# Experts' rows by indexed DMA through a table in memory, in place of gather and scatter matmuls

## The chip, the cores and the metric

One core of a Trainium2 chip runs the whole program. The metric is the device time of one execution, in microseconds. PE is the matrix engine, DVE the vector engine, ACT the scalar engine, POOL the general engine that here clears buffers and issues small loads, SP the engine that issues the weight loads. Each engine runs its own list of instructions in order and waits for the others through semaphores.

## The reference

Two layers over 256 frames of width 1024. Each has a token mixer and a channel mixer; the channel mixer of the second layer is a top-2-of-8 expert SwiGLU, and that is where the change lies:

```python
logits = (xf @ w_router) + b_router
top_logit, top_idx = lax.top_k(logits, 2)
top_w = softmax(top_logit)
# for every expert e, over the rows routed to it:
out = (silu(xb @ w1[e]) * (xb @ w3[e])) @ w2[e]      # 1024 -> 3584 -> 1024
y[token] += out * weight_of_that_row                  # each token is in two experts
x = layer_norm(alpha * x + (1 + gate) * y)
```

There are 512 routed rows in all; how many an expert gets is known only on the chip.

## The kernel before, in words

**Weights.** All weights stream from memory in pieces of 1 MB (w_raw, a ring of 6) on SP's queue. For each piece ACT rounds a high part (w_hi, L755 in the expert stage, L498 before) and DVE subtracts to get the low part (w_lo, L1300, or L878); both have 3 slots, freed when PE has used the piece (split_used). A product is three matmuls, high by high, low by high, high by low (L1426 to L1428). A ring slot is free again once DVE has made the low part (piece_used).

**Experts.** The stream of one expert is 42 pieces: 7 panels of A (w1), B (w3) and C (w2), two pieces each. The three engines run a loop over 8 experts and branch on the expert's row count: over 192 rows, 129 to 192 ("packed"), 65 to 128, and up to 64 ("few"). Up to 128 rows are one block, more are two. In the packed and few forms the low part of a 64-row half sits in the partitions 64 to 127 beside the high part, so that one matmul serves both, and the sums of both halves are added later. For C this is the product of L1432 and L1433; an expert of 65 to 128 rows has the extra matmuls of L1953.

**Rows in and out.** The normalised rows are kept as h_hi and h_lo. DVE builds 0/1 matrices (pick, L1268, and pick_w with the routing weight, L1269). PE gathers the rows of a block with 16 products from h_hi and 16 from h_lo (L1871), which come out turned as the next operand; ACT and DVE copy them to actT_hi (L741) and actT_lo (L1276). After an expert ACT and DVE copy its sums to hbuf (L845, L1385); early in the next expert, between its second and third piece, PE scatters them with 8 matmul instructions per block (L1880), and DVE adds the result to yacc (L1284). pick_w is turned on PE (L1914) to place. An expert opens its 2 or 4 sum banks with products of zeros (L1944), after its fourth piece.

**Order around the change.** At an expert's end PE runs: turn of the last panel (L1925), gather for the next expert (L1871), wait for gT (ACT L779, then DVE L1323 or L1327), the last two C pieces, and, next expert, A, A, scatter, B, turn of pick_w, B, zeros. The order is written out by hand in each engine's program; nothing is planned at run time but the branches on the count.

**The start of the program.** In the first token mixer every second piece is a modulation piece, which DVE multiplies into mod_acc (L905). mod_acc is first cleared by POOL (L441 to L443) and gets its bias by a small load on POOL's queue (L449); the first modulation piece waits for that load (semaphore acc_ready). DVE takes pieces in the order of the stream.

Of the kernel before, what the change touches and what calls it, by code (L numbers as in the profile page):

```python
# [23 lines left out]
F32 = mybir.dt.float32  # L24
# [38 lines left out]
CONSTS = C_IOTA + SEQ  # L63


def constants():

    c = np.zeros((P, CONSTS), np.float32)
# [118 lines left out]
DVE_MIX_STEPS, DVE_DENSE_STEPS, DVE_ROUTE_STEPS = 39, 22, 32  # L187
# [16 lines left out]
def trunk(nc, I, consts, out):  # L204
    with ExitStack() as ctx:
# [52 lines left out]
        h_lo = sb("h_lo", [P, TT, D], F32R, scope=ffn)  # L258
        h_hi = sb("h_hi", [P, TT, D], F32R, scope=ffn)
# [6 lines left out]
        pick = sb("pick", [P, TT, SEQ], F32R, scope=ffn)  # L266
# [6 lines left out]
        wsel = sb("wsel", [P, TT, EXPERTS + 1], scope=ffn)  # L273
        ffn.close()

        ps = ctx.enter_context(nc.psum_tensor("ps", [P, 8, BANK], F32))

        gT_end_hi, gT_end_lo = (h_hi[:, part, 0:BANK].rearrange("p (b c q) -> p b c q", b=2, q=P) for part in range(2))
# [23 lines left out]
        acc_free, acc_zero, yacc_zero = sem("acc_free"), sem("acc_zero"), sem("yacc_zero")  # L302
# [30 lines left out]
        hh_ready, hl_ready = sem("hh_ready"), sem("hl_ready")  # L333
# [4 lines left out]
        gathered_hi = [sem(f"gathered_hi{b}") for b in range(2)]  # L338
        gathered_lo = [sem(f"gathered_lo{b}") for b in range(2)]
# [98 lines left out]
        def _(gp):  # L438
# [20 lines left out]
            gp.dma_start(cst[:, C_PAST:], consts[:, C_PAST:]).then_inc(tables_loaded, 16)  # L459
            for layer in range(DEPTH):  # L460
# [29 lines left out]
        def _(act):  # L490
# [58 lines left out]
            def route_norms(sub, n, held, ahead):  # L549

                def high_h(t):
                    A(h_hi[:, t, :], hbuf[:, t, :], ACT.Copy).then_inc(hh_ready, 1)

# [7 lines left out]
                high_h(0)  # L561
                root(n + 4, 1)
                ahead(2)
                keep_turned(sub, 1, held)
                high_h(1)
# [14 lines left out]
            for layer in range(DEPTH):  # L580
# [149 lines left out]
                else:  # L730
# [8 lines left out]
                    def gathered_rows(b, n, first_bank=4):  # L739
                        act.wait_ge(gathered_hi[b], n)  # L740
                        A(actT_hi[:, :, b * P:(b + 1) * P],  # L741
                          ps[:, first_bank:first_bank + 2, :].rearrange("p c (k q) -> p (c k) q", q=P), ACT.Copy).then_inc(xg_hi_ready[b], 1)

                    gathered_rows(0, 1)
                    with nc.Fori(0, EXPERTS, engines=[act.engine], hint_back_edge=True, head_slot={act.engine: 0}) as e:
                        count = act.value_load(counts_i[0:1, bass.ds(e, 1)], min_val=0, max_val=SEQ)

                        def expert(blocks, packed=False, few=False):
# [33 lines left out]
                            def places():  # L782
                                act.wait_ge(place_sent, e + 1)
                                ins = A(place[:, 0:blocks, :], ps[:, 0, 0:blocks * SEQ].rearrange("p (b q) -> p b q", q=SEQ), ACT.Copy)
                                if packed or few:
                                    half = blocks - 1
                                    ins.then_inc(place_copied, 1)
                                    act.wait_ge(place_copied, e + 1)
                                    ins = A(place[HALF_P:P, half, :], ps[0:HALF_P, 0, half * SEQ:(half + 1) * SEQ], ACT.Copy)
                                else:  # L790
                                    act.sem_inc(place_copied, 1)
# [4 lines left out]
                            if blocks == 2:  # L796
                                gathered_rows(1, e + 1)
                            else:
                                act.sem_inc(xg_hi_ready[1], 1)
# [5 lines left out]
                            places()  # L805
# [27 lines left out]

                            def tail(last):
                                gT_part(panel_0 + NP)
                                if not last:
                                    round_at(12, loads6, done6)
                                    if blocks == 1:
                                        gathered_rows(0, e + 2, 6)
                                    round_at(13, loads6, done6)  # L840
                                    if blocks == 1:
                                        round_at(14, loads6, done6)
                                act.wait_ge(split_used, done0 + (EXPERT.n_split + SPLIT))
                                for b in range(blocks):
                                    ins = A(hbuf[:, b, 0:BANK], bank(2 * b), ACT.Copy)  # L845
                                ins.then_inc(y_act, 1)
                                if not last and blocks == 2:
                                    round_at(14, loads6, done6)
                                    gathered_rows(0, e + 2)
# [21 lines left out]
        def _(dve):  # L871
# [157 lines left out]
            dve.sem_inc(added, 4)  # L1029
# [12 lines left out]
            for layer in range(DEPTH):  # L1042
# [173 lines left out]
                else:  # L1216
# [3 lines left out]
                    def low_h(t):  # L1220
                        dve.wait_ge(hh_ready, t + 1)
                        TTn(h_lo[:, t, :], hbuf[:, t, :], h_hi[:, t, :].bitcast(F32), ALU.subtract).then_inc(hl_ready, 1)

                    low_h(0)
                    rest_of_piece(EXPERT, 0, sbase + MIX.n_split)
                    wide = [P, TT, EXPERTS]
# [18 lines left out]
                    TTn(gap, m2, m1, ALU.subtract).then_inc(gap_ready, 1)  # L1245
                    dve.wait_ge(e2_ready, 1)
# [3 lines left out]
                    step(TTn(tmp, is1, w1.broadcast_to(wide), ALU.mult))  # L1250
                    step(TTn(is2, is2, w2.broadcast_to(wide), ALU.mult))

                    nc.vector.memset(wsel[:, :, EXPERTS:], 0.0)
                    nc.vector.memset(posm[:, :, EXPERTS:], -1.0)
                    step(TTn(wsel[:, :, 0:EXPERTS], tmp, is2, ALU.add))
                    low_h(1)
                    dve.wait_ge(pos_sent, 1)

                    step(STT(pos, ps[:, ROUTE + 1, 0:16].rearrange("p (t e) -> p t e", t=TT), 1.0, sel, ALU.add, ALU.mult))
                    step(TS(posm[:, :, 0:EXPERTS], pos, -1.0, None, ALU.add))  # L1260
                    nc.vector.tensor_copy(counts_i[:, 0:EXPERTS], ps[:, ROUTE + 1, 16:24]).then_inc(counts_ready, 1)
# [3 lines left out]
                    def pick_tokens(e):  # L1265
                        for t in range(TT):
                            at = posm[:, t, bass.ds(e, 1)]
                            TS(pick[:, t, :], iota, at, None, ALU.is_equal)  # L1268
                            ins = TS(pick_w[:, t, :], iota, at, wsel[:, t, bass.ds(e, 1)], ALU.is_equal, ALU.mult)  # L1269
                        ins.then_inc(pick_ready, 1)  # L1270
# [3 lines left out]
                    def gathered_rows(b, n, first_bank=6):  # L1274
# [775 lines left out]
```

## Time and profile before

| | us |
|---|---|
| three runs | 1778.58, 1779.21, 1779.35 |
| median | 1779.21 |
| span of the profiled execution | 1779.2 |

| engine | busy us | share of the span |
|---|---|---|
| PE | 1695.2 | 95% |
| DVE | 1375.4 | 77% |
| ACT | 1026.8 | 58% |
| POOL | 36.7 | 2% |

The page gives no other time for the profiled execution than its span, which is that of the median run. In this view a matmul's busy time overlaps the next one's, so a run of n matmuls is read from the start of the first to the start of what follows. Waits are put down to the semaphore that came last. The DMA share is the busy share of the core's 16 DMA engines.

### The profile page before, as it was taken

The numbers are of one execution on the slowest core, as the hardware profiler recorded it, in microseconds if no ns is written. First come the engines' busy times: TensorE is split into PE (matmuls) and PEld (weight loads), VectorE is DVE, ScalarE is ACT, GpSimd is POOL, SyncE is SP. The second block draws the span as 40 slices with busy tenths as digits, with TensorE's granted clock in tenths as the row PEclk, the third lists the DMA queues.
The fourth block names the chain that finished last, engine by engine and source line by source line (L and its number), as shares of the span: only waits on it lengthen the run. The fifth ranks groups of instructions, "written<-read, shape, count | busy, mean of one in ns | idle before, by whom it ended". The sixth has DMA issues, their size and how long they took to land.

```text
span 1779.2 us, 21351 instructions
## 1 busy us (share of the span) xinstructions
PE 1695.2 (95%) x7542; PEld 1306.9 (73%) x7543; DVE 1375.4 (77%) x1171; ACT 1026.8 (58%) x823; POOL 36.7 (2%) x40
## 2 busy tenths in 40 slices
PE   5999899999999898999999999999899999999995
PEld 2587758887677766777877778887677777787773
DVE  5686868676786886888888966656488889888887
ACT  1375433433465335777767765454477777777772
POOL 1100010000100000000000000000000000000000
PEclk9999999999999998999999999999999999999998
DMA  9885459774685246999999976666499999999992
GB/s 358 306 319 180 154 180 333 279 260 142 245 295 172 97 175 243 384 377 339 369 329 342 386 285 214 212 213 234 138 371 394 335 378 385 336 370 359 341 379 84
DMA packets 210530, 502.24 MB, mean 282 GB/s; under 512 B 9137, under 2 KB 13409, under 8 KB 210481
## 3 DMA queue, kind: packets, MB, share of 16 engines
q1 hardware_dynamic: 208770, 496.15, 77.5%
q0 software_dynamic: 1712, 5.43, 1.0%
q8 instruction: 32, 0.52, 0.1%
q14 instruction: 16, 0.13, 0.0%
HBM read 500.50 MB, written 1.05 MB: 282 GB/s over the span
## 4 chain that ended last, share of the span: by engine, by line
PE 84%; DVE 9%; issue 4%; DMA 2%; ACT 1%; DVEq 0%; SPq 0%; ACTq 0%
PE ps L1426 20%; PE ps L1428 19%; PE ps L1427 19%; PE ps L1432 5%; PE ps L1433 5%; PE ps L1437 4%; DVE w_lo L1300 3%; PE ps L1880 2%; PE ps L1953 2%; PE ps L1871 2%; PE ps L1925 2%; DMA w_raw<-in_w_mod_mix_dram 1%; DVE gates L1095 1%; DMA w_raw<-in_w_in_dram 1%; PE ps L1488 1%
## 5 line engine op out<-in xcount | busy, mean ns | idle before, releaser
L1300 DVE TENSOR_TENSOR w_lo<-w_raw,w_hi 128x2048 fp32r<-128x2048 f32 x333 | 757.9, 2290 | 197.3 <-ACT w_hi L755 195.4
L755 ACT CAST w_hi<-w_raw 128x2048 fp32r<-128x2048 f32 x333 | 635.9, 1910 | 199.7 <-PE ps L1433 107.3
L1426 PE MATMUL ps<-w_hi,actT_hi 128*128 128x512 f32 (+1 forms) x1464 | 584.2, 399 | 31.7 <-issue 11.2
L1428 PE MATMUL ps<-w_hi,actT_lo 128*128 128x512 f32 (+1 forms) x1464 | 567.3, 387 | 0.0
L1427 PE MATMUL ps<-w_lo,actT_hi 128*128 128x512 f32 (+1 forms) x1464 | 566.8, 387 | 0.0
L1426 PEld LDWEIGHTS ps<-w_hi,actT_hi 128*128 128x128 f32 x1464 | 277.0, 189 | 103.4 <-issue 26.6
L1428 PEld LDWEIGHTS ps<-w_hi,actT_lo 128*128 128x128 f32 x1464 | 276.9, 189 | 57.6
L1427 PEld LDWEIGHTS ps<-w_lo,actT_hi 128*128 128x128 f32 x1464 | 277.5, 190 | 55.2 <-issue 3.3
L878 DVE TENSOR_TENSOR w_lo<-w_raw,w_hi 128x2048 fp32r<-128x2048 f32 x81 | 185.4, 2290 | 91.3 <-ACT w_hi L498 91.0
L498 ACT CAST w_hi<-w_raw 128x2048 fp32r<-128x2048 f32 x81 | 154.5, 1909 | 112.0 <-PE ps L1428 98.8
L1432 PE MATMUL ps<-w_hi,gT_hi 128*128 128x512 f32 x448 | 183.3, 409 | 4.7 <-issue 1.9
L1433 PE MATMUL ps<-w_lo,gT_hi 128*128 128x512 f32 x448 | 177.1, 395 | 0.0
L905 DVE SCALAR_TENSOR_TENSOR mod_acc<-w_raw,c_act,mod_acc 128x512 f32<-128x512 f32 x176 | 120.1, 747 | 10.5 <-DMA w_raw<-in_w_mod_mix_dram 10.5
L1432 PEld LDWEIGHTS ps<-w_hi,gT_hi 128*128 128x128 f32 x448 | 84.1, 188 | 43.7 <-issue 26.3
L1433 PEld LDWEIGHTS ps<-w_lo,gT_hi 128*128 128x128 f32 x448 | 84.2, 188 | 17.6
L1437 PE MATMUL ps<-w_raw,actT_raw 128*128 128x512 f32 x144 | 66.4, 617 | 4.8 <-DMA w_raw<-in_w_in_dram 4.0
L1437 PEld LDWEIGHTS ps<-w_raw,actT_raw 128*128 128x128 f32 x144 | 27.9, 197 | 39.5 <-issue 37.4
L1426 PE MATMUL ps<-w_hi,gT_hi 128*128 128x512 f32 x136 | 54.1, 398 | 2.2 <-DVE gT_hi L1327 2.2
L765 ACT ACTIVATE silu<-ps 128x512 f32<-128x512 f32 x56 | 33.5, 599 | 39.2 <-PE ps L1428 38.9
L1427 PE MATMUL ps<-w_lo,gT_hi 128*128 128x512 f32 x136 | 54.1, 398 | 0.0
L1428 PE MATMUL ps<-w_hi,gT_lo 128*128 128x512 f32 x136 | 53.5, 393 | 0.0
L779 ACT ACTIVATE gT_hi<-ps 128x256 fp32r<-128x256 f32 (+1 forms) x63 | 27.9, 453 | 37.0 <-PE ps L1925 37.0
(249 smaller groups left out, 1283.9 us busy)
## 6 DMA issues: line engine op xcount, KB each, us to landing
w_raw<-in_exp_w_dram SPq DMA_DIRECT2D x336, 1024.0 KB, 5.9
w_raw<-in_ffn_w_dram SPq DMA_DIRECT2D x33, 1024.0 KB, 5.3
w_raw<-in_w_mod_mix_dram SPq DMA_DIRECT2D x24, 1024.0 KB, 9.2
w_raw<-in_w_mod_ffn_dram SPq DMA_DIRECT2D x24, 1024.0 KB, 5.7
w_raw<-in_w_gate_dram SPq DMA_DIRECT2D x24, 1024.0 KB, 6.8
w_raw<-in_w_in_dram SPq DMA_DIRECT2D x14, 1024.0 KB, 6.4
w_raw<-in_w_out_dram SPq DMA_DIRECT2D x8, 1024.0 KB, 5.1
w_raw<-in_w_branch_c_dram SPq DMA_DIRECT2D x4, 1024.0 KB, 5.0
```

What stands on the lines that cost most here:

```text
L498: nc.scalar.copy(w_hi[:, j % SPLIT, :], w_raw[:, i % RING, :]).then_inc(split_hi, 1)
L755: nc.scalar.copy(w_hi[:, i % SPLIT, :], w_raw[:, i % RING, :]).then_inc(split_hi, 1)
L878: TTn(w_lo[:, j % SPLIT, :], w_raw[:, i % RING, :], w_hi[:, j % SPLIT, :].bitcast(F32), ALU.subtract).then_inc(piece_used, 1)
L905: ins = STT(acc, w[:, k, n * BANK:(n + 1) * BANK], c_act[:, 2 * (q % 4) + k:2 * (q % 4) + k + 1], acc, ALU.mult, ALU.add)
L1300: TTn(w_lo[:, i % SPLIT, :], w_raw[:, i % RING, :], w_hi[:, i % SPLIT, :].bitcast(F32), ALU.subtract).then_inc(piece_used, 1)
L1426: MM(to, hi, w_h, start=first, stop=False)
L1427: MM(to, hi, w_l, start=False, stop=False)
L1428: return MM(to, lo, w_h, start=False, stop=last)
L1432: MM(to, packed, w_h, start=first, stop=False)
L1433: return MM(to, packed, w_l, start=False, stop=last)
L1437: return MM(to, actT_raw[:, k, t * P:(t + 1) * P], w_raw[:, slot, at * width:(at + 1) * width], start=first, stop=last)
L1871: ins = MM(to, part[:, t, k * P:(k + 1) * P], pick[:, t, b * P:(b + 1) * P], start=t == 0, stop=t == 1)
```

## The change

- The rows no longer go through pick, h_hi and h_lo. A table by_row in memory (8 experts by 256 rows of 4 KB) takes each token's row once per chosen expert by 4 indexed DMAs from POOL; the row numbers are computed on DVE (row_no, row_at). An expert's rows are then loaded to xrows by two plain DMAs, and PE turns them with 8 transposes per block (turn_rows); ACT makes the high part and DVE the low part by subtraction.
- At the end of each expert but the last, the sums go to hbuf (for few and packed experts both halves are added there, through fold), and ACT issues the DMA that writes them into the same places of by_row (send_rows). After the last expert has begun, POOL fetches them with 4 indexed DMAs to yacc and xrows; DVE multiplies them by the routing weights w1 and w2. Only the last expert's rows go through place and the scatter matmuls.
- The whole table is first cleared: 16 DMAs of 512 KB each, from a block of zeros in the constants, issued by POOL before the first mixer's small loads.
- The first routing steps on DVE are reordered, PE's filler products after the count are 10 and not 2, the filler after the last expert's turn is gone, and PE waits for the rows inside the branch on the count.

On POOL, at the start of the program; cst and by_row are loaded from the constants, mod_acc's is the bias load. Before:

```order
L459 DMA cst<-constants_dram 128x1984
L462 DMA sinks_sb<-in_sinks_dram 128x8
L463 DMA pool_scale_sb<-in_pool_scale_dram 128x2x1
L466 DMA w_pool_sb<-in_w_pool_dram 64x2x64 x2
L449 DMA mod_acc<-in_b_mod_ffn_dram 1x16x192
```

And now, with the 16 clearing DMAs:

```order
L468 DMA cst<-constants_dram 128x1984 [waits piece_used]
L470 DMA by_row<-constants_dram 128x1024 x16
L473 DMA sinks_sb<-in_sinks_dram 128x8 [waits gate1_ready]
L474 DMA pool_scale_sb<-in_pool_scale_dram 128x2x1
L477 DMA w_pool_sb<-in_w_pool_dram 64x2x64 x2
L458 DMA mod_acc<-in_b_mod_ffn_dram 1x16x192 [waits acc_zero]
```

The clears stand ahead of every small load of the first mixer in the same queue (the three memsets between the last two rows are left out in both lists).

On PE, at the end of an expert of one block, from the turn of the last panel (gated) to the first matmuls of the tenth piece. Before:

```order
L1925 MATMUL ps<-cst,gated 128x128 x4
L1871 MATMUL ps<-pick,h_hi 128x128 x16
L1871 MATMUL ps<-pick,h_lo 128x128 x16
L1467 MATMUL ps<-cst 128x512 x3
L1953 MATMUL ps<-w_hi,gT_lo 128x512 x4
L1432 MATMUL ps<-w_hi,gT_hi 128x512
```

And now:

```order
L1984 MATMUL ps<-cst,gated 128x128 x4
L1938 MATMUL ps<-cst,xrows 128x128 x8
L1973 MATMUL ps<-cst,pick_w 128x128 x2
L2013 MATMUL ps<-w_hi,gT_lo 128x512 x4
L1502 MATMUL ps<-w_hi,gT_hi 128x512
```

32 gather matmuls give way to 8 transposes; the third row is the branch of the last expert in both, filler before, the turn of pick_w now.

On ACT, at the end of a few expert; raw_loaded2 stands at the rounding of the next expert's third piece. Before:

```order
L754 REGISTER_ALU [waits raw_loaded2]
L755 CAST w_hi<-w_raw 128x2048 [waits split_used]
L845 ACTIVATE hbuf<-ps 128x512 [waits split_used]
L851 UNCONDITIONAL_BRANCH
```

And now:

```order
L786 REGISTER_ALU [waits raw_loaded2]
L787 CAST w_hi<-w_raw 128x2048 [waits split_used]
L866 ISA [waits rows_sent]
L873 ACTIVATE fold<-ps 64x512 [waits split_used,y_sent_rows]
L873 ACTIVATE fold<-ps 64x512
L882 ISA [waits y_act,y_dve]
L882 DMA by_row<-hbuf 64x1024
L899 UNCONDITIONAL_BRANCH
```

One copy becomes two, and ACT now stands still for DVE (y_dve) and issues a DMA before it goes on to the next expert's pieces.

The diff, cut to its core:

```diff
@@
-DVE_MIX_STEPS, DVE_DENSE_STEPS, DVE_ROUTE_STEPS = 39, 22, 32
+DVE_MIX_STEPS, DVE_DENSE_STEPS, DVE_ROUTE_STEPS = 39, 22, 40
...
+        by_row = nc.dram_tensor("by_row", (EXPERTS * SEQ, D), F32).ap()
@@ block.gpsimd
-            gp.dma_start(cst[:, C_PAST:], consts[:, C_PAST:]).then_inc(tables_loaded, 16)
+            gp.dma_start(cst[:, C_PAST:], consts[:, C_PAST:CONSTS]).then_inc(tables_loaded, 16)
+            for n in range(EXPERTS * TT):
+                gp.dma_start(by_row[n * P:(n + 1) * P, :], consts[:, C_ZERO:C_ZERO + D]).then_inc(rows_cleared, 16)
             for layer in range(DEPTH):
...
-                    nc.gpsimd.memset(yacc[:, :, :], 0.0).then_inc(yacc_zero, 1)
                     nc.gpsimd.memset(zeros[:, :].bitcast(F32), 0.0).then_inc(zeros_set, 1)
-                    for b in range(2):
-                        gp.wait_ge(gathered_lo[b], EXPERTS)
-                    ln_rows(I["ln_ffn_g"][1], I["ln_ffn_b"][1])
+                    gp.wait_ge(rows_cleared, EXPERTS * TT * 16)
+                    gp.wait_ge(h_ready, 16)
+                    gp.wait_ge(row_at_ready, 1)
+                    for c in range(2):
+                        for t in range(TT):
+                            gp.indirect_dma_start(out=by_row[:, :], out_offset=bass.IndirectOffsetOnAxis(ap=row_at[:, c, t, :], axis=0),
+                                                  in_=hbuf[:, t, :], in_offset=None).then_inc(rows_sent, 16)
+                    gp.wait_ge(rows_sent, 4 * 16)
+                    for e in range(EXPERTS):
+                        if e:
+                            gp.wait_ge(turned[1], e)
+                            gp.wait_ge(rows_loaded[1], e * 16)
+                        for b in range(2):
+                            gp.dma_start(xrows[:, b, :], by_row[e * SEQ + b * P:e * SEQ + (b + 1) * P, :]).then_inc(rows_loaded[b], 16)
+                        if e == 0:
+                            ln_rows(I["ln_ffn_g"][1], I["ln_ffn_b"][1])
...
+                    for c, to in enumerate((yacc, xrows)):
+                        for t in range(TT):
+                            gp.indirect_dma_start(out=to[:, t, :], out_offset=None, in_=by_row[:, :], ...).then_inc(y_gathered, 16)
@@ block.scalar
+                    def turned_rows(b, n):
+                        act.wait_ge(turned[b], n)
+                        for c in range(2):
+                            ins = A(actT_hi[:, 4 * c:4 * c + 4, b * P:(b + 1) * P], bank(HW3 + 2 * c)..., ACT.Copy)
+                        ins.then_inc(xg_hi_ready[b], 1)
...
+                            def copy_sums(folds):
+                                act.wait_ge(rows_sent, 4 * 16)
+                                act.wait_ge(y_sent_rows, e * 32 + 32)
+                                act.wait_ge(split_used, done0 + (EXPERT.n_split + SPLIT))
+                                half = blocks - 1
+                                for b in range(half if folds else blocks):
+                                    ins = A(hbuf[:, b, 0:BANK], bank(2 * b), ACT.Copy)
+                                if folds:
+                                    for c in range(2):
+                                        ins = A(fold[:, c, :], ps[HALF_P:P, 2 * half + c, :], ACT.Copy)
+                                ins.then_inc(y_act, 1)
+                            def send_rows():
+                                act.wait_ge(y_dve, e + 2)
+                                act.wait_ge(y_act, e + 2)
+                                for b in range(blocks):
+                                    n = HALF_P if few or b and packed else P
+                                    act.dma_start(by_row[bass.ds(act.snap(e * SEQ + b * P), n), :], hbuf[0:n, b, :]).then_inc(y_sent_rows, 16)
@@ block.vector
+                            def copy_sums(folds):
...
+                                if folds:
+                                    dve.wait_ge(y_act, e + 2)
+                                    for c in range(2):
+                                        ins = TTn(hbuf[0:HALF_P, half, c * BANK:(c + 1) * BANK], fold[:, c, :], ps[0:HALF_P, 2 * half + c, :], ALU.add)
+                                ins.then_inc(y_dve, 1)
...
+                                rest_at(12, done6)
+                                turned_rows(0, e + 2)
+                                rest_at(13, done6)
+                                copy_sums(packed or few)
+                                rest_at(14, done6)
...
-                    add_rows(EXPERTS)
+                    dve.wait_ge(y_gathered, 4 * 16)
+                    for t in range(TT):
+                        ins = TS(yacc[:, t, :], yacc[:, t, :], w1[:, t, :], None, ALU.mult)
+                    step(ins)
+                    for t in range(TT):
+                        ins = STT(yacc[:, t, :], xrows[:, t, :], w2[:, t, :], yacc[:, t, :], ALU.mult, ALU.add)
+                    step(ins)
...
@@ block.tensor
-                    stay_busy(2, 3)
-                    pe.wait_ge(hh_ready, TT)
-                    pe.wait_ge(hl_ready, TT)
+                    stay_busy(10, 3)
                     pe.wait_ge(counts_ready, 1)
+                    def turn_rows(b, n):
+                        pe.wait_ge(rows_loaded[b], n * 16)
+                        for k in range(KD):
+                            ins = TR(ps[:, HW3 + 2 * (k // 4), ...], xrows[:, b, k * P:(k + 1) * P], ident)
+                        ins.then_inc(turned[b], 1)
...
                             turn(panel_0 + NP)
-                            if blocks == 1:
-                                with pe.If(e < EXPERTS - 1):
-                                    pe.wait_ge(pick_ready, e + 2)
-                                    gather(0, e + 2, 6, 2)
-                                with pe.Else():
-                                    stay_busy(3, 6)
+                            with pe.If(e < EXPERTS - 1):
+                                turn_rows(0, e + 2)
+                            with pe.Else():
+                                turn_places()
```

## Rows read from the trace of the kernel before

**Rows 1.** The page, the chain that ended last, its shares by engine.

```profile
PE 84%; DVE 9%; issue 4%; DMA 2%; ACT 1%; DVEq 0%; SPq 0%; ACTq 0%
```

**Rows 2.** Stretch of one few expert: us, busy per engine, clock, DMA share, GB/s.

```profile
924.00:1045.00 121.00, 118.06 (x542) 92.64 (x540) 106.19 (x67) 91.36 (x64) 0.00 (x0) 1.00 0.99 362
```

**Rows 3.** Groups by line, the packed low part of gT on DVE.

```profile
L1327 DVE TENSOR_TENSOR gT_hi<-ps,gT_hi 128x256 fp32r<-128x256 f32 x42 | 17.6, 418 | 0.0
```

**Rows 4.** Timeline of POOL, 50 to 70 us: start, duration, operation, wait before.

```profile
51.34 0.53 POOL L459 DMA_DIRECT2D cst<-constants_dram  x1 [43.65 <-DVE mod_acc L905]
...
67.62 0.52 POOL L449 DMA_DIRECT2D mod_acc<-in_b_mod_ffn_dram  x1 [0.29 <-POOL mod_acc L443]
```

**Rows 5.** DMA queues between 52 and 64 us: packets, MB, share of 16 engines.

```profile
q1 hardware_dynamic: 634, 1.42, 31.3%
q0 software_dynamic: 272, 1.09, 25.2%
```

**Rows 6.** PE and DMA in the first mixer, 80 to 90 us, as in Rows 2.

```profile
80.00:90.00 10.00, 10.00 (x54) 1.00 1.04 399
```

**Rows 7.** Timeline of SP, first and last load issued before 72.4 us.

```profile
64.29 0.37 SPq L390 DMA_DIRECT2D w_raw<-in_w_mod_ffn_dram  x1
...
71.57 0.47 SPq L390 DMA_DIRECT2D w_raw<-in_w_in_dram  x1
```

**Rows 8.** Timeline of DVE and PE at the first modulation piece of the mixer.

```profile
72.44 2.73 DVE L905 SCALAR_TENSOR_TENSOR mod_acc<-w_raw,c_act,mod_acc 128x512 f32<-128x512 f32 x4
75.09 2.28 DVE L878 TENSOR_TENSOR w_lo<-w_raw,w_hi 128x2048 fp32r<-128x2048 f32 x1
...
76.45 1.03 PE L1616 MATMUL ps<-cst,proj 128*128 128x128 f32 x8
77.43 0.50 PE L1426 MATMUL ps<-w_hi,actT_hi 128*128 128x512 f32 x1
```

**Rows 9.** PE at the start of the experts: a timeline row, then the stretch after.

```profile
673.99 0.79 PE L1426 MATMUL ps<-w_hi,actT_hi 128*128 128x512 f32 x1 [5.71 <-issue]
...
674.00:679.70 5.70, 5.70 (x13) 0.50 0.01 3
```

**Rows 10.** Timeline at the end of a few expert and the start of the next.

```profile
1381.63 1.98 PE L1871 MATMUL ps<-pick,h_hi 128*128 128x128 f32 x16
...
1385.23 0.45 PE L1432 MATMUL ps<-w_hi,gT_hi 128*128 128x512 f32 x1
...
1383.90 0.42 DVE L1327 TENSOR_TENSOR gT_hi<-ps,gT_hi 128x256 fp32r<-128x256 f32 x1
...
1391.03 0.60 ACT L845 ACTIVATE hbuf<-ps 128x512 f32<-128x512 f32 x1
1391.65 1.28 ACT L755 ACT_TABLE_LOAD   x1
1392.94 1.92 ACT L755 CAST w_hi<-w_raw 128x2048 fp32r<-128x2048 f32 x1
...
1394.51 3.60 PE L1880 MATMUL ps<-hbuf,place 128*128 128x512 f32 x8
...
1404.14 0.39 PE L1426 MATMUL ps<-w_hi,actT_hi 128*128 128x512 f32 x1
```

**Rows 11.** Timeline after the packed expert: PE begins the next one, then scatters.

```profile
1264.04 0.79 PE L1426 MATMUL ps<-w_hi,actT_hi 128*128 128x512 f32 x1 [5.51 <-issue]
...
1271.06 7.03 PE L1880 MATMUL ps<-hbuf,place 128*128 128x512 f32 x16
```

**Rows 12.** Timeline of PE after a 65 to 128 row expert: the next one begins its fifth piece.

```profile
936.59 0.39 PE L1426 MATMUL ps<-w_hi,actT_hi 128*128 128x512 f32 x1
```

**Rows 13.** Timeline of DVE at the end, and groups of like operations by line.

```profile
1761.36 0.69 DVE L1284 TENSOR_TENSOR yacc<-yacc,ps 128x512 f32<-128x512 f32 x1 [0.17 <-PE ps L1880]
...
L953 DVE SCALAR_TENSOR_TENSOR x_sb<-hbuf,rstd,lnrow 128x1024 f32<-128x1024 f32 x8 | 10.3, 1285 | 0.3
...
L1117 DVE TENSOR_SCALAR z_sb<-z_sb 128x1536 f32<-128x1536 f32 x2 | 1.9, 960 | 0.1
```

More of the change, by code:

```diff
@@ L273, in trunk @@
         wsel = sb("wsel", [P, TT, EXPERTS + 1], scope=ffn)
+        row_no = sb("row_no", [P, 8, TT, 1], scope=ffn)
+        row_at = sb("row_at", [P, 4, TT, 1], I32, scope=ffn)
         ffn.close()
+        by_row = nc.dram_tensor("by_row", (EXPERTS * SEQ, D), F32).ap()
         ps = ctx.enter_context(nc.psum_tensor("ps", [P, 8, BANK], F32))
-        gT_end_hi, gT_end_lo = (h_hi[:, part, 0:BANK].rearrange("p (b c q) -> p b c q", b=2, q=P) for part in range(2))
+        gT_end_hi, gT_end_lo = (gT_end[:, part, :].rearrange("p (b c q) -> p b c q", b=2, q=P) for part in range(2))
         assert 2 * DENSE_PANELS[-1] == BANK
@@ L337, in trunk @@
         pick_ready, place_sent, place_ready = sem("pick_ready"), sem("place_sent"), sem("place_ready")
-        gathered_hi = [sem(f"gathered_hi{b}") for b in range(2)]
-        gathered_lo = [sem(f"gathered_lo{b}") for b in range(2)]
+        turned = [sem(f"turned{b}") for b in range(2)]
         xg_hi_ready = [sem(f"xg_hi_ready{b}") for b in range(2)]
@@ L787, in places @@
                                     ins.then_inc(place_copied, 1)
[L788 to L791, printed above, removed]
+                                    act.wait_ge(place_copied, 1)
+                                    ins = A(place[HALF_P:P, half, :], ps[0:HALF_P, HW3, half * SEQ:(half + 1) * SEQ], ACT.Copy)
                                 ins.then_inc(place_ready, 1)
@@ L843, in tail @@
[L843 to L849, printed above, removed]
+                                if last:
+                                    places()
+                                    copy_sums(False)
+                                    return
@@ L1027, in _ @@
                 statistics(chain, x, t)
-            dve.sem_inc(added, 4)
             for t in range(TT):
@@ L1245, in _ @@
                     TTn(gap, m2, m1, ALU.subtract).then_inc(gap_ready, 1)
+                    dve.wait_ge(pos_sent, 1)
+                    row1, row2, off1, off2, to1, to2, was1, was2 = (row_no[:, n] for n in range(8))
+                    step(STT(pos, ps[:, ROUTE + 1, 0:16].rearrange("p (t e) -> p t e", t=TT), 1.0, sel, ALU.add, ALU.mult))
+                    step(STT(rest, number, float(SEQ), pos, ALU.mult, ALU.add))
+                    TTn(logit, is1, rest, ALU.mult)
+                    step(TTn(tmp, is2, rest, ALU.mult))
+                    RED(row1, logit, AX_X, ALU.add)
+                    step(RED(row2, tmp, AX_X, ALU.add))
+                    TS(row_at[:, 0], row1, -1.0, None, ALU.add)
+                    TS(row_at[:, 1], row2, -1.0, None, ALU.add).then_inc(row_at_ready, 1)
+                    nc.vector.tensor_copy(counts_i[:, 0:EXPERTS], ps[:, ROUTE + 1, 16:24]).then_inc(counts_ready, 1)
+                    rest_of_piece(EXPERT, 2, sbase + MIX.n_split)
                     dve.wait_ge(e2_ready, 1)
@@ L1262, in _ @@
+                    TS(row_at[:, 2], to1, -1.0, None, ALU.add)
+                    TS(row_at[:, 3], to2, -1.0, None, ALU.add).then_inc(y_at_ready, 1)
+                    TS(off1, was1, -1.0, 1.0, ALU.mult, ALU.add)
+                    step(TS(off2, was2, -1.0, 1.0, ALU.mult, ALU.add))
+                    TTn(w1, w1, off1, ALU.mult)
+                    step(TTn(w2, w2, off2, ALU.mult))
                     dve.wait_ge(counts_ready, 1)
                     moe_splits = LAYER_SPLITS + MIX.n_split
[L1265 to L1270, printed above, removed]
```

204 lines of the change are left out of this document (95 added, 109 removed).

## The prediction

> **What bounds the kernel now.** I read the chain of waits first. It runs through PE for 84% of the span [rows 1]: what comes off PE, and is not taken over by another wait, comes off the time. The granted clock and DMA share of an expert come next. In a few expert PE is busy throughout at full clock, yet the 16 DMA engines are 99% busy at 362 GB/s [rows 2]: matrix engine and weight stream end almost together. Six of the eight experts make the packed low part (42 groups over 7 panels [rows 3]); one of them is the packed one, the fourth in the timeline, so five are few and two have 65 to 128 rows. Last come the timelines of the places that the change touches: the experts' ends, where gather and scatter stand; the start of the experts; the end; and, far from the experts, the first mixer, where the 16 clearing DMAs now stand in POOL's queue.
>
> **1. The clears (the largest loss).** POOL issues its table load at 51.34 us in 0.53 us [rows 4]. Sixteen clears at about that price keep it until 60.4, so the bias load leaves near 68.9 and not at 67.6. POOL's own time is small. But the bias load stands behind 8.39 MB in one queue, and DVE's first modulation piece, at 72.44 [rows 8], waits for it. What the DMA engines must move from 52 us until then: 1.42 MB on SP's queue and 1.09 on POOL's that were moved anyway by 64 us [rows 5], the 8.39 of the clears, and the four weight pieces that SP issues between 64.29 and 71.57 [rows 7], 4.19. More weights cannot be asked for, since their slots come free behind the stalled DVE. That is 15.1 MB. At the 399 GB/s of a saturated stretch of this mixer [rows 6] it takes 37.8 us, until 90. I take 90 for the bias to land; 90 − 72.4 is 17.5 us.
> Nothing covers it. The low part that follows the modulation piece on DVE ends at 75.09 + 2.28 = 77.4, and PE's next piece begins at 77.43 [rows 8], with no slack, while PE is 10.0 of 10 us busy afterwards [rows 6], so it has nowhere to make it up. After such a pause PE comes back slow: in the experts' first stretch it had stood 5.7 us and was granted 0.50, the 1.2 GHz level, for 5.7 us [rows 9], which is 2.7 us of work lost. Sum of this step: +20. Bounds: 0, if the bias need not wait for the clears; 30, if memory-to-memory copies run at 300 GB/s instead of 399 (no row shows such a copy).
> No row tells in which order one queue is served. The Trainium skill (DMA: Bandwidth & Descriptors, section Queues, rings and completion order) says that each DMA engine takes the descriptors of a queue in ring order and alternates between queues by packets. By it the bias stays behind all clears and the step costs what stands above; were it not so, the step would be 0, which is the first rival.
>
> **2. The start of the experts.** Before, the gathers ended at 668.3, and PE then stood 5.71 us on "issue" until 673.99 [rows 9], with the new code of the loop. Now row_at is ready at about 660.5. Four indexed DMAs follow; the trace has none. Lower bound for each is the direct 0.53 us [rows 4]; I take twice that, 4.2 us for four, and for writing the last 0.52 MB 1.3 us at 399 GB/s plus an estimated 2.4 for the way: 668.5. Loading the first block back is 0.5 + 1.3 + 2.4: 672.7. Eight transposes take 1.03 us warm [rows 8], 2 cold; then the loop's code, 5.7 us again: 680.4, against 674.0. Less DVE's and ACT's parts, which fit under the code: +6. Bounds: 0 (the code comes early) and +15 (each indexed DMA takes 3 us).
>
> **3. The experts' ends, where the gain is.** Per boundary PE loses a gather, from 1381.63 until the C pieces begin at 1385.23, 3.6 us, for 1.0 us of transposes; a scatter, 3.60 less its overlapped tail of 0.6; and the turn of places, 0.3 [rows 10]. Before, these covered ACT and DVE. Between two few experts, where I follow it piece by piece:
> - gT's low part ends at 1383.90 + 0.42 = 1384.3 [rows 10]; PE, done with its transposes at 1382.9, waits. C begins at 1384.4: 0.8 of 2.6 gained.
> - C ends at 1388.05. ACT rounds the third piece (1.9) until 1390.3, copies two halves (0.6 each [rows 10]) until 1391.5, and waits for DVE's two adds, 0.69 each [rows 13], until 1392.9. Behind that wait stand its DMA issue (0.4), the table load (1.28) and the fourth piece (1.92) [rows 10]: 1396.5. Silu with its table load gives 1398.4, the fifth piece 1400.3, its low part on DVE (2.28 [rows 8]) 1402.6.
> - PE begins its fifth piece there; before it was 1404.14 [rows 10]. Gain 1.5 us of 5.8 taken off PE.
> After an expert of 65 to 128 rows ACT's copy is one, and DVE copies beside it without waiting. The same steps put the fifth piece at 932.3 and not 936.59 [rows 12]: 4.3. After the packed expert the gather stood between the sums and the 5.51 us "issue" [rows 11]; gather 4.3, scatter of two blocks 7.03 less 0.6, and places go in full: 11. Before the packed expert ACT's blocked copies come ahead of the second block's turned rows, and PE waits 6.8 us for them: gather and scatter gone, gain 1.
> Sum: 3 × 1.5 + 2 × 4.3 + 11 + 1 = 25. Bounds: all that PE is spared, 17.5 for seven gathers, 2.5 for the second block's, 24 for eight blocks' scatters, 2 for places, is 46, if ACT and DVE follow at once; 13 if every boundary but the packed one's gives only its 0.3. I take 25, near the middle, as the chains above are the rows' own.
>
> **4. Traffic.** Each expert adds 1.05 MB of rows in (both blocks always) and 0.26 to 0.8 out; at a DMA share of 0.99 [rows 2]. At an expert's head there is room while PE waits, so I take 2 us over five few experts; bounds 0 and 8 (1.3 MB by 5 at 399 GB/s is 16 us, of which the heads hide half).
>
> **5. The end.** DVE's adds ended at 1761.36 + 0.69 [rows 13], right behind PE's scatter. Now they come after two scalings (1024 columns by the 960 ns of 1536 [rows 13], 0.64 each) and two multiply-adds (1.285 each), 3.9 us, which begin with the copies done at 1757.1: 1761.1, and four adds of 0.69 end at 1763.9. Cost +2. The fetch of the rows itself starts when the last expert does, seven panels ahead.
>
> **Sum.** +20 + 6 − 25 + 2 + 2 = +5. The profiled span is 1779.2, the same as the median of the runs: 1784 us.
>
> **The rivals.**
> - *The clears hide.* The bias lands among them, or copies leave the weight queue its share, and step 1 is 0 to 4. For it: the weight queue is not busy around 60 us (1.42 MB in 12 us is 118 GB/s [rows 5]), which leaves room for some 3 MB. Against: 8.39 MB do not fit in it. Then −25 + 10 + 2 is −13: 1766, faster.
> - *ACT and DVE follow at once.* The boundaries give 40 and not 25, the clears as forecast: 1769. Against it, the chain of rows 10 has ACT's wait for DVE ahead of the fourth piece.
> - *Memory writes are slow.* The clears run at 300 GB/s or less (+30), and each indexed DMA takes 3 us (+15), the boundaries as forecast: 1779 + 30 + 15 − 25 + 4 = 1803. It decides from a clear of 1.7 us per 512 KB on.
> - *The stream of weights becomes the bound in few experts.* 45.4 MB at 399 GB/s is 114 us; they last 121 − 1.5. It would need under 380 GB/s, where 362 was moved at a 0.99 share [rows 2]: then nothing is gained there, 4.5 us less: 1789.
>
> **Chances.** Forecast 0.48 (own range 1776 to 1792), clears hidden 0.19, boundaries in full 0.10, slow writes 0.13, stream bound 0.10. Within 0.2%, 3.6 us, a measurement of this kernel can tell no change. Faster takes the first and second rival and 0.05 of the forecast's, 0.34; the same 0.11, from the forecast's lower edge; slower the rest, 0.55. Range 1764 to 1801.
>
> **What would show it.** A wait of DVE's first modulation piece on the small load near 72 us until 90, POOL's queue full of copies meanwhile, and PE at the 1.2 GHz level after it, show step 1; no such wait makes the prediction wrong and the time near 1766. PE's first expert matmul near 700 (674 + 20 + 6) shows steps 1 and 2 together. In a few expert's head, "w_hi waits for DVE" with PE waiting for w_lo at its third to fifth piece shows step 3; boundaries that shrink by 5 us make it wrong. Waits for w_raw in the expert stage would be step 4. After the last scatter DVE must be found in adds that begin 2 us later.

## The result: 45 us slower, where 5 were predicted

| | before | changed |
|---|---|---|
| median us | 1779.28 | 1824.80 |
| lowest and highest of 4 runs | 1778.58, 1781.82 | 1821.98, 1825.76 |
| profiled span | 1779.2 | 1823.9 |
| PE busy, us | 1695.2 | 1667.4 |
| PE's share of the chain of waits | 84% [rows 1] | 74% |

The ratio is 1.0248 (95% interval 1.0236 to 1.026). PE's busy time falls by 28 us, and the time rises by 45. The chain that ended last, in the profile after, by engine:

```profile
PE 74%; DVE 12%; issue 7%; DMA 3%; ACT 2%; POOL 1%; ACTq 0%; DVEq 0%; SPq 0%; POOLq 0%
```

"Issue", time in which an engine waits for nothing that the profile shows, grew from 4% to 7%, DVE from 9% to 12%. To see where, I put the two timelines side by side at marks that both have, and take the differences of their starts:

| stretch, and its mark | before | after | added us | predicted |
|---|---|---|---|---|
| up to the counts on DVE (counts_i) | 660.42 | 685.18 | 24.8 | 20 |
| start of the experts, to their first matmul | 673.99 | 710.02 | 11.3 | 6 |
| the eight experts, to the copy of the last sum | 1756.81 | 1799.61 | 6.8 | −25 + 2 |
| the end, to the end of the span | 1779.2 | 1823.9 | 1.9 | 2 |

Three rows of four are within 6 us of the forecast. The third is off by 30.

**The first mixer, after.** DVE's modulation piece of [rows 8], which started at 72.44 without a wait, in the timelines of DVE and PE:

```profile
93.46 2.74 DVE L953 SCALAR_TENSOR_TENSOR mod_acc<-w_raw,c_act,mod_acc 128x512 f32<-128x512 f32 x4 [22.24 <-DMA mod_acc<-in_b_mod_ffn_dram]
...
98.46 0.79 PE L1496 MATMUL ps<-w_hi,actT_hi 128*128 128x512 f32 x1 [22.28 <-DVE w_lo L926]
```

And the stretches, with columns as in [rows 2]:

```profile
80.00:90.00 10.00, 0.00 (x0) 0.00 (x0) 0.00 (x0) 2.88 (x3) 0.00 (x0) 0.53 1.01 388
90.00:100.00 10.00, 1.54 (x4) 1.25 (x5) 6.54 (x8) 2.88 (x3) 0.00 (x0) 0.50 0.44 142
```

Between 80 and 90 us PE does nothing, where it was 10.0 us busy [rows 6], while the DMA engines move about as much as before (388 GB/s for 399). The bias load is issued at 67.96 and lands 25.5 us later, against 3.4 in the kernel before. ACT stands too: it waits for two weight pieces, 12.8 us until 82.12 and 9.7 us until 94.70. PE then comes back at a granted clock of 0.50, the 1.2 GHz level.

**The start of the experts, after.** Timeline of POOL and PE:

```profile
686.18 2.24 POOL L500 DMA_INDIRECT by_row<-hbuf,row_at  x1 [11.28 <-DVE row_at L1299]
...
691.28 0.95 POOL L500 DMA_INDIRECT by_row<-hbuf,row_at  x1 [0.30 <-issue]
...
699.16 1.14 POOL L509 DMA_DIRECT2D xrows<-by_row  x2 [6.93 <-DMA by_row<-hbuf,row_at]
...
702.83 1.94 PE L1938 MATMUL ps<-cst,xrows 128*128 128x128 f32 x8 [10.15 <-DMA xrows<-by_row]
...
710.02 0.79 PE L1496 MATMUL ps<-w_hi,actT_hi 128*128 128x512 f32 x1 [5.26 <-issue]
```

Each step of the predicted chain is there, in its order. Four indexed stores take 6.1 us, from 686.18 to 692.23 (I took 4.2), the last lands 6.9 us later (3.7), and the load back takes 3.7 (4.2). The "issue" of [rows 9] stays.

**An expert's end, after.** The first boundary, where a few expert ends, in the timeline:

```profile
832.29 1.08 ACT L873 ACTIVATE fold<-ps 64x512 f32<-64x512 f32 x2
833.48 1.28 DVE L1437 TENSOR_TENSOR hbuf<-fold,ps 64x512 f32<-64x512 f32 x2 [0.78 <-ACT fold L873]
...
838.28 1.28 ACT L787 ACT_TABLE_LOAD   x1 [4.91 <-issue]
...
841.50 2.29 DVE L1353 TENSOR_TENSOR w_lo<-w_raw,w_hi 128x2048 fp32r<-128x2048 f32 x1 [4.55 <-ACT w_hi L787]
...
843.85 0.50 PE L1496 MATMUL ps<-w_hi,actT_hi 128*128 128x512 f32 x1 [3.83 <-DVE w_lo L1353]
```

ACT ends its copies at 833.37 and begins nothing until 838.28. Before, it went from its copy straight into the table load (1391.03 + 0.60 and 1391.65, at another few expert's end [rows 10]). Of the 4.9 us only 1.4 are DVE's adds, which end at 834.76. ACT's late piece makes DVE's low part late and that makes PE late. ACT's waits on "issue" in the experts' part:

```profile
ACT L787 <- issue: 31.0, 7, 5.8
ACT L770 <- issue: 4.8, 1, 4.8
```

The columns are us in total, times, longest. One of the seven of L787, 4.6 us, is the first expert's entry; the other six and the one of L770 are the seven boundaries, 31.2 us. PE's waits for its first pieces there are 5.05, 2.67, 9.48, 6.91, 5.04, 4.62 and 3.03 us, in all 36.8; before they were 1.40 and 5.51, at the third and fourth boundary, and nothing at the others. Two of them, 6.91 and 5.04, are PE's own "issue" and not ACT's doing; they come up again below.

DVE is not always the one that ACT waits for. After an expert of 65 to 128 rows DVE's copy ends first (962.52 at the second boundary, ACT's own at 962.88), and ACT still begins nothing for 2.86 us after its own, and for 3.19 at the seventh boundary. The instruction in front of the store waits for `y_act` as well as `y_dve`, that is, for the end of ACT's own copy.

### The profile page after: what moved, and what is told of

It is laid out like the page before. It is cut to its first block, busy times and chain, and to the rows that moved or that the text cites. A ratio compares the mean times of both kernels' runs of the same rounds, so it can differ in the third digit from the quotient of the medians.

```text
span 1823.9 us, 20741 instructions
## 1 busy us (share of the span) xinstructions
PE 1667.4 (91%) x7256; PEld 1283.5 (70%) x7257; DVE 1356.1 (74%) x1144; ACT 1022.5 (56%) x823; POOL 64.2 (4%) x79
## 4 chain that ended last, share of the span: by engine, by line
PE 74%; DVE 12%; issue 7%; DMA 3%; ACT 2%; POOL 1%; ACTq 0%; DVEq 0%; SPq 0%; POOLq 0%
PE ps L1496 19%; PE ps L1497 18%; PE ps L1498 18%; DVE w_lo L1353 4%; PE ps L1502 4%; PE ps L1503 4%; PE ps L1507 2%; PE ps L2013 1%; DMA mod_acc<-in_b_mod_ffn_dram 1%; PE ps L1984 1%; DMA w_raw<-in_w_mod_mix_dram 1%; DVE w_lo L926 1%; DVE mod_acc L953 1%; ACT w_hi L787 1%; DVE gates L1142 1%
## 5 line engine op out<-in xcount | busy, mean ns | idle before, releaser
L787 ACT CAST w_hi<-w_raw 128x2048 fp32r<-128x2048 f32 x333 | 635.0, 1910 | 202.8 <-PE ps L1503 109.9
L1507 PEld LDWEIGHTS ps<-w_raw,actT_raw 128*128 128x128 f32 x144 | 27.5, 194 | 38.9 <-issue 36.8
```

What stands on the lines that cost most here:

```text
L787: nc.scalar.copy(w_hi[:, i % SPLIT, :], w_raw[:, i % RING, :]).then_inc(split_hi, 1)
L1507: return MM(to, actT_raw[:, k, t * P:(t + 1) * P], w_raw[:, slot, at * width:(at + 1) * width], start=first, stop=last)
```

## The experiments

Each is timed beside the kernel before on its own chip (1780.0 to 1780.6 there), so differences of about 1 us to the changed kernel tell nothing.

**The clears alone.** The kernel before, with the table, its source of zeros and this, behind the load of the constants:

```diff
+            for n in range(EXPERTS * TT):
+                gp.dma_start(by_row[n * P:(n + 1) * P, :], consts[:, C_ZERO:C_ZERO + D]).then_inc(rows_cleared, 16)
```

> The kernel before with nothing changed but the 16 clears at 51.6 us. If they are the whole of the first 25.2 us, it takes 1779.3 + 25 = 1804 us, and the experts' part is as long as before. If half of that belongs to something else in the change, 1790 us or less.

Measured: 1804.75 us, ratio 1.0136 (1.0119 to 1.0153), 24.7 above the kernel before. The eight experts take 1081.9 us there against 1082.8. So step 1 is the clears and nothing else.

**The same clears, directly behind the bias load.** In the changed kernel:

```diff
-            for n in range(EXPERTS * TT):
-                gp.dma_start(by_row[...], consts[...]).then_inc(rows_cleared, 16)
...
                 fresh_acc(I["b_mod_ffn"][bass.ds(layer, 1), :], layer * 2 + 1)
+                if layer == 0:
+                    for n in range(EXPERTS * TT):
+                        gp.dma_start(by_row[...], consts[...]).then_inc(rows_cleared, 16)
```

> The same clears at the same place in the program, but issued just after the bias load instead of just before it. If the order in the queue costs the time (the small load waits behind 16 bulk copies), the 22.2 us wait of mod_acc goes and the time is 1800 to 1803 us. If it is the bandwidth that the clears take from the weight loads between 68 and 110 us, the wait turns into waits for w_raw and the time stays over 1815 us.

Measured: 1818.46 us (1.0196 to 1.023), 6.3 less than the changed kernel. DVE waits for no bias, yet the mark of the first mixer's end (the load of lnrow, 215.74 before) is at 236.13, 20.4 late. Its waits, in the stretch from 50 to 240 us:

```profile
ACT w_hi L532 <- DMA w_raw<-in_w_in_dram: 21.2, 2, 18.7
...
ACT w_hi L532 <- DMA w_raw<-in_w_gate_dram: 9.7, 1, 9.7
```

In the kernel before these two are 3.6 and 3.1 us. The bias lands in 3.6 us now, behind nothing, and the weights are late; in the changed kernel ACT's waits for in_w_in were 22.5 us too, hidden beside DVE's wait for the bias. So the second expectation held: it is the 8.39 MB at this moment that cost, in whichever order.

**The clears at the same point of the second layer**, `if layer == 1` in place of `if layer == 0`.

> The changed kernel with its 16 clears of the table issued at 481 us instead of 51.6 us, behind the second layer's bias load, where the DMA engines are about half idle. If the loss of the first 130 us is the clears standing ahead of the bias load, all 25.2 us of it go: 1799.6 us, lnrow load back near 215.7 us. If clears cost their traffic wherever they are (16.8 MB read and written, some 40 us of all engines), most of it comes back later: 1815 us or more.

Measured: 1819.02 us (1.02 to 1.0234). The time is that of the second expectation, over 1815, but its reason, that clears cost their traffic wherever they stand, falls with the next run. The clears leave at 457.1 us and not at 481; the next mark, 611.24 before, is at 629.15, 17.9 late, and the waits from 440 to 690 us say why (3.5 us on this line before):

```profile
ACT w_hi L532 <- DMA w_raw<-in_w_in_dram: 28.8, 2, 15.7
```

I had chosen the place by the 40 slices of the page of before, where the slice from 445 to 490 us moves 245 GB/s at six tenths of the share. A slice averages a pause with a rush: the same kernel moves 8 GB/s from 445 to 455 us and 393 from 475 to 490, which are the mixer's first weights.

**The clears in the middle of the first mixer's gates.** This time chosen from 10-us stretches of the kernel before, where 140 to 200 us moves 119 to 213 GB/s and 200 to 210 nothing:

```diff
+                if layer == 0:
+                    gp.wait_ge(split_used, SPLIT + 13)
+                    for n in range(EXPERTS * TT):
+                        gp.dma_start(by_row[...], consts[...]).then_inc(rows_cleared, 16)
                 gp.wait_ge(merged_ready, layer * 4 + 4)
```

> The changed kernel with the 16 clears issued at about 147 us, in the middle of the first layer's gates, where the kernel before moves 190 GB/s and less until 210 us, and is halfway between two bias loads. Clears at 457 us had cost 17.6 us and clears just behind the bias load 20.4 us, both by starving the weight loads of the stretch that follows (367 to 399 GB/s with them). If it is the stretch that makes them dear, nearly all of the 25 us goes here: 1799 to 1803 us. If 8.4 MB of clears cost some 20 us wherever they are put, it stays at 1815 to 1820 us.

Measured: 1799.07 us (ratio 1.0089 to 1.012), 25.7 less than the changed kernel. The clears left at 134.4 and not 147, and cost nothing: the mark of 215.74 is at 214.45, although the DMA engines move 338 to 407 GB/s from 140 to 180 us. No engine waits longer for a load there than before (ACT 3.7 and 2.7 us from 50 to 240 us, against 3.6 and 3.1); that the ring's slots hold enough weights by then is my reading and was not tried by itself.

**Half of the clears in the old place, half in the free one** (they leave from 141.7 us on).

> The changed kernel with 8 of the 16 clears at 51.6 us and the other 8 at 134 us, where 16 had cost nothing. If the loss is in proportion to the clears ahead of the bias load and of the weight loads, half of the 25 us is left: 1811 to 1813 us, and mod_acc waits some 10 us for its load. If the first few clears are free because the engines have room at 51 to 70 us (136 GB/s in the kernel before), it is 1800 to 1805 us.

Measured: 1808.78 us (1.0137 to 1.0177), 9.7 above the version with all sixteen moved. That lies between the two expectations. By the times and by the mark (223.05), the first eight cost 7 to 10 us, the second eight 16 to 18, and DVE waits 2.7 us for the bias where 10 were expected. So part of them does fit into the free room around 60 us, which was the first rival.

**The stores of the sums by POOL.** ACT's wait, for DVE and for its own copy, and its DMA issue are gone; POOL, idle there, waits for both halves and issues the store (the count is read and the four sizes told apart on POOL, and a new semaphore gives hbuf back).

```diff
-                                act.wait_ge(y_dve, e + 2)
-                                act.wait_ge(y_act, e + 2)
-                                for b in range(blocks):
-                                    act.dma_start(by_row[...], hbuf[0:n, b, :]).then_inc(y_sent_rows, 16)
...
+                        gp.wait_ge(y_dve, e + 2)
+                        gp.wait_ge(y_act, e + 2)
+                            gp.dma_start(by_row[...], hbuf[r:r + n, b, :]).then_inc(y_sent_rows, 16)
+                        gp.wait_ge(y_sent_rows, (e + 1) * 32)
+                        gp.sem_inc(y_free, 1)
```

> The changed kernel, but GpSimd, which is idle there, waits for the experts' sums and issues the seven stores of them; ScalarE no longer waits for VectorE nor issues a DMA at an expert's end. If ScalarE's halt of about 4.9 us at each of the seven ends makes VectorE and then TensorE late, TensorE's waits for w_lo and actT_hi at the ends (5.1, 2.7, 9.5, 4.6 and 3.0 us) go and the time falls by 20 to 28 us, to 1797 to 1805. If the few-row experts are already at the DMA engines' ceiling (369 GB/s at a busy share of 1.00), their part is not gained: a fall of 8 to 15 us. If TensorE's and ScalarE's halts are both late program code, nothing changes: 1822 to 1826.

Measured: 1800.67 us (1.0091 to 1.0135), 24.1 less than the changed kernel, within the first expectation. The same boundary as above, timeline:

```profile
831.14 1.08 ACT L902 ACTIVATE fold<-ps 64x512 f32<-64x512 f32 x2
832.24 1.28 ACT L816 ACT_TABLE_LOAD   x1
832.33 1.28 DVE L1455 TENSOR_TENSOR hbuf<-fold,ps 64x512 f32<-64x512 f32 x2 [0.75 <-ACT fold L902]
...
834.45 0.99 POOL L512 DMA_DIRECT2D by_row<-hbuf  x2 [122.14 <-DVE hbuf L1455]
```

ACT's halt of 4.91 is 0.02 us, as it is at all seven boundaries, and PE's waits there fall from 36.8 to 19.3 us. PE's busy time falls too, by 7.3 us to 1660.1, for the same matmuls: after the halts that are gone it no longer runs at the low clock. Together that is 24.8 us, about the 24.1. The ceiling rival fell too: the third expert (a few one) takes 119 us here and moves 383 GB/s, where it took 124 at 369.

**The wait without the issue.** The last version, with ACT waiting again but issuing nothing:

```diff
                                 copy_sums(packed or few)
+                                act.wait_ge(y_dve, e + 2)
+                                act.wait_ge(y_act, e + 2)
+                                act.sem_inc(y_seen, 1)
```

> The version with the stores issued by GpSimd (1800.7 us), in which ScalarE still waits for VectorE's sums at an expert's end, but issues no DMA. If the wait alone makes ScalarE late (registers, the count and the branch then follow it instead of running ahead), its halt is 4 us or more at the seven ends again and the time goes back to 1815 to 1825. If the halt was the DMA issue, the halt is 1.5 us and the time 1800 to 1806.

Measured: 1812.94 us (1.0162 to 1.0193), so 12.3 of the 24.1 come back, between the two expectations; its four runs spread over 10 us (1808.48 to 1818.44). Same boundary:

```profile
832.09 1.27 DVE L1458 TENSOR_TENSOR hbuf<-fold,ps 64x512 f32<-64x512 f32 x2 [0.76 <-ACT fold L902]
...
835.48 1.28 ACT L816 ACT_TABLE_LOAD   x1 [3.50 <-issue]
```

DVE's adds end at 833.36, and ACT still begins only 2.1 us later with no DMA to issue. What it does there is the loop's end: registers, the next count, the branches. The trace has the sequencer's read of the count (`counts_i`), without the wait and with it:

```profile
L807 ACTq TENSOR_LOAD <-counts_i x1: 296/296/296, 830.1 to 830.1; - x1
...
L807 ACTq TENSOR_LOAD <-counts_i x1: 296/296/296, 834.2 to 834.2; - x1
```

Without the wait the count is read at 830.1, while ACT's unit still rounds a piece (until 831.1), as in the kernel before (794.5, rounding until 795.7). With it the count is read 0.85 us after DVE's adds, and the unit stands. From the end of what ACT waited for to its next instruction it is 1.8 to 2.2 us at all seven boundaries, also at the two where that was its own copy. The seven halts sum to 21.6 us, with the issue to 31.2, without either to 0.1. So 3.5 of the 4.9 us belong to the wait, 1.4 to the issue. Which of the two waits, `y_dve` or `y_act`, would be enough was not tried at the few experts' ends; at the two experts of 65 to 128 rows DVE was done before.

**Both mends together.**

> Clears at 147 us and the stores of the experts' sums issued by GpSimd, together. If the two losses are separate, 1824.8 - 25 - 24 = 1776 us, 3 to 4 us faster than the kernel before. If they share a cause (the stores and clears fall on the same queue), 1785 us or more.

Measured: 1773.35 us, ratio 0.996 (0.9946 to 0.9973): 51.5 less than the changed kernel, and 6.7 us, or 0.4%, faster than the kernel before. This is the fastest version of the case with the second block still loaded for every expert.

**Less traffic.** In that version:

```diff
                         for b in range(2):
+                            n = P if b == 0 or e == 3 else 16
-                            gp.dma_start(xrows[:, b, :], by_row[...]).then_inc(rows_loaded[b], 16)
+                            gp.dma_start(xrows[0:n, b, :], by_row[...]).then_inc(rows_loaded[b], 16)
```

> The version with both changes, in which the second block of rows is loaded in full only for the one expert of this input that needs it, and 16 rows of it for the others: 3.2 MB less of loads during the experts. If the few-row experts are at the ceiling of the DMA engines (busy share 1.00), each gains 1.2 us, some 7 us in all against the version with both changes. If TensorE sets their length, under 2 us.

Measured: 1772.79 us (0.9942 to 0.9972), 0.6 less, within the spread of either. The 7 us of a DMA ceiling are refuted. Step 4's 2 us is not, and its upper bound of 8 isn't settled either: this took away less than a third of the traffic that the change added.

**PE's own halt.** At the entry of the sixth expert PE stands 5.0 us on "issue" in the changed kernel and 5.1 in the version with both mends, where the kernel before does not stand at all:

```profile
1387.27 0.79 PE L1516 MATMUL ps<-w_hi,actT_hi 128*128 128x512 f32 x1 [5.06 <-issue]
```

In the changed kernel PE's waits for the rows stand behind the branch on the count, in each arm; this version puts them back in front of it.

> The version with both changes, with TensorE's two waits for an expert's rows back in front of the branch on the count, as in the kernel before, instead of behind it. TensorE still halts 5.1 us on nothing that the profile shows at the entry of the sixth expert, which the kernel before did not. If the place of the waits makes that halt, it goes and the time is 1768 us. If it is program code that arrives late whatever the waits, 1772 to 1775 us as before.

Measured: 1775.70 us (0.9962 to 0.9983), and the halt is there, 3.86 us. It isn't the place of the waits. PE's sequencer has a record of what it does meanwhile. In the version with both mends, the branch on the count at the sixth expert's entry, and the DMA queue of the program's own instructions from 1380 to 1387 us:

```profile
L2083 PEldq COMPARE_BRANCH  x1: 6712/6712/6712, 1380.2 to 1380.2; - x1
...
q8 instruction: 2, 0.03, 2.3%
```

One branch takes 6.71 us; the same branch at the seventh expert's entry takes 0.22, and that queue moves nothing there. In every trace of this case PE's branches of over 1 us (3.4 to 7.8) have one or two such packets within them, the 5.51 us of [rows 11] too. So PE waits at a branch while program code is loaded. Why the changed program has one more such place than the one before is open.

## Why the prediction was wrong

- **Step 1, the clears: right in kind, 20 for 25.** The wait that I named came, on the load that I named, until 93.5 in place of 90. Its mechanism was told too narrowly: I held all of it to be the bias standing behind the clears, and wrote that without that order the step would be 0. The clears just behind the bias cost 20.4. The Trainium skill's rule on the order within a queue (DMA: Bandwidth & Descriptors, section Queues, rings and completion order) is borne out by the bias load: 25.5 us from issue to landing behind 16 clears, 3.6 ahead of them. It only didn't decide the price.
- **Step 2, the start: +6 for +11.3.** The chain was right, and its unknown, the indexed store, was mis-sized: 6.1 us of issue and 6.9 until it landed, against 4.2 and 3.7. It lay within the bounds of 0 and 15. The 2.4 us "for the way" that the sum has twice stand in no row; the load back, where they are one term of 4.2, took 3.7.
- **Step 3, the experts' ends: this step failed**, −25 for about +5 to +7. What failed is one sentence of it: "Behind that wait stand its DMA issue (0.4), the table load (1.28) and the fourth piece". I had the wait, its end and what is queued behind it on the engine as busy work. I left out what never shows as busy: the loop's registers, the read of the count and the branches. In the kernel before, ACT did all that while its unit was still at the copies (a gap of 0.02 us at the boundary), so no busy row prices it; only the time of its reads of the count shows that it was hidden. Once ACT waits just ahead of the loop's end, for DVE or for the end of its own copy, it does them afterwards, in the open: 3.8 us from the end of DVE's adds to ACT's next instruction at a late boundary (1428.10 to 1431.93), 3.5 at the first, where I had 0.4.

  After an expert of 65 to 128 rows I wrote that DVE copies "without waiting" and forecast a gain of 4.3; ACT waited for its own copy, and nothing was gained.

  The seven halts are 31.2 us of ACT's time, and the version without wait and issue gives 24.1 of the run's time back: in its trace the eight experts take 1065.9 us, against 1089.6 and 1082.8 before. That is −17; with PE's halt at the sixth expert (5 us) it would be −22. From one expert's products of zeros to the next one's, that version gains 2.5, 4.8, −1.3, 9.6, −3.0, 2.5 and 4.9 us at the seven boundaries, where I had 1.5, 4.3, 1, 11, 1.5, 1.5 and 4.3. So the gains were real, the packed expert's even in the changed kernel (9.9), and the halts ate the others. Its last expert takes 4.5 us more than before, which no run takes apart.
- **Step 4: neither shown nor refuted.** Taking 3.2 MB away gave 0.6 us. **Step 5: right**, 1.9 for 2.
- **The rivals.** None held. "The clears hide" needed the room that half of the clears found in part. "Memory writes are slow" would have given 1803 by way of the first two steps alone. All four kept step 3 as a gain, of 20 at the least, so the range ended at 1801, though the step's own lower bound was 13 and nothing in it allowed for a loss. A wait newly put on ACT at each of seven boundaries was a rival in its own right. I priced its wait for DVE and an issue of 0.4 us, and nothing behind them.

## What to carry to other kernels

A wait put just ahead of a loop's end or a branch, for another engine or for the engine's own last operation, costs more than the time it waits: all that the engine's sequencer used to do in the shadow of its unit then follows it in the open, and no busy row shows that work. Look for the gap between the last instruction before the branch and the first one behind it, and for the time at which the sequencer reads the loop's count; where the gap is near nothing, the work of the branch is hidden, and a wait there brings it out. Give such waits to an engine that is idle.

Bulk copies go where stretches of 10 us show room; half empty slices of the profile's page can hide a full rush, and here the cost wasn't avoided by mending the order in the queue. An "issue" wait of PE at a branch can be told by its sequencer's record: a branch of several us, with packets on the instruction queue.

## What the runs showed of the hardware

- Sixteen copies from memory to memory, 8.39 MB, made the next mark 25.3 us late when they left at 51 us of the program, 20.4 at 68, 17.9 at 457, and not late at all at 134. In the last case too the DMA engines were 98 to 104% busy, at 338 to 407 GB/s, until 180 us.
- An indexed store of 128 rows of 4 KB takes 2.24 us to issue the first time and 0.95 to 0.99 us after, against 0.53 to 0.57 for a direct one, and lands in a median of 7.6 us.
- A wait of ACT's sequencer ahead of this loop's end costs 1.8 to 2.2 us beyond the wait, and 1.4 more in the mean where it issues a DMA there with an address from a register (31.2 against 21.6 us over seven).
- The branch on the count takes PE's sequencer 0.09 to 0.23 us at most experts' entries, and 6.1 to 7.8 us at the sixth one's in the ten versions of the changed kernel traced, with packets of the instruction queue within it.
- In the changed kernel, after the halt at each of the seven boundaries (2.7 us or more) PE was granted 0.50 to 0.57 over the next 3 to 5 us (0.72 at the first boundary). At the sixth expert's entry a matmul takes 0.63 to 0.64 us from 1428.7 until 1432.1, the 1.2 GHz level, then 0.39.
